# Summing the experts' rows into x by small products on chip, in a one-core decoder layer with 32 experts

## The chip, the core and the metric

The kernel runs on one core of a Trainium2 chip, as one program. The metric is the device time of one execution in microseconds (us); the number that counts is the median of several runs. The profile is of one further execution.

## What is computed

One inference step of a decoder layer for 264 tokens (256 of a prompt, 8 samples) with 1024 channels: a projection, an RWKV-7 branch and an attention branch, their merge into `x`, and then a layer of experts. Each token goes to 4 of 32 experts, and the 4 results, weighted, are added to `x`; a last norm gives `y`. The first part is not touched by the change. The second, cut to what matters, with all numbers in float32:

```python
def clamped_swiglu(u):
    glu = jnp.minimum(u[..., :D_FF], SWIGLU_LIMIT)
    lin = jnp.clip(u[..., D_FF:], -SWIGLU_LIMIT, SWIGLU_LIMIT)
    return glu * jax.nn.sigmoid(SWIGLU_ALPHA * glu) * (lin + 1.0)
...
    logits = (x @ w_router).astype(jnp.float32) + b_router.astype(jnp.float32)
    top_val, top_e = lax.top_k(logits, TOP_K)
    top_w = jax.nn.softmax(top_val, axis=-1).astype(h.dtype)
...
    def expert_chunk(args):
        xc, e = args
        return clamped_swiglu(xc @ w_up[e] + b_up[e]) @ w_down[e] + b_down[e]
    ys = lax.map(expert_chunk, (xs, chunk_e)).reshape(slots, D_MODEL)
    out = jax.ops.segment_sum(ys * slot_w[:, None], slot_tok, num_segments=n + 1)[:n]
...
    return x + moe_ffn(rms_norm(x, norm_ffn), w_router, b_router, w_up, b_up, w_down, b_down)
...
    y_prompt = rms_norm(xp, norm_final)
    y_sample = rms_norm(xs, norm_final)
```

Each expert has an upper weight of 1024x2048 (8 MB) and a lower one of 1024x1024 (4 MB).

## The kernel before

The engines run programs of their own and meet at semaphores. The layer of experts has four blocks of code, one behind the other, with all engines meeting between them.

`route` norms `x`, finds the 4 experts of each token, and gives each (token, choice) a slot: 64 slots to an expert (`SLOTS`), and further tiles of 64 for experts with more tokens, up to 16. A product with one-hot matrices (`hit`, `cell`) turns this into a table of slots by tiles; `src_row` has the row of the normed `h` (in memory) that a slot reads, `dst_row` the row of `scratch["choice"]` (also in memory, 4 rows to a token) that it writes. A row is handled as two halves of 512 elements, so a tile of 64 slots by 1024 channels is 128 partitions by 512. `route` also loads the biases, the first upper weight and the first two lower ones.

`first_tiles` goes through the 32 experts. SyncE streams the weights into `ring`: 8 slots of 1 MB for the upper weight, which are refilled as soon as TensorE has used them (`up_used`), and 2 x 4 slots for the lower ones (`down_used`). GpSimd gathers the rows of the next expert by an indirect transfer (`gather`), and writes the result of the last one by another (`scatter`). TensorE's order is written out by hand:

```python
with pe.Fori(1, NEXP // 2) as pair:
    up(2 * pair, True)
    turn_x(2 * pair + 1)
    down(2 * pair - 1, pair - 1, 1, True)
    up(2 * pair + 1, True)
    turn_x(2 * pair + 2)
    down(2 * pair, pair, 0, True)
```

`up(e)` multiplies the 64 rows by the 8 chunks of the upper weight (`L2039`), each into both column halves of the array, with `turn_h(e - 1)` (`L2026`) ahead of chunk 4, and adds the bias by a product of a one-hot `pick_up` with the bias table (`L2045`). `turn_x` (`L2020`) transposes the gathered rows. `down` multiplies by the lower weight (`L2057`) and adds its bias (`L2062`). VectorE's `tile(e)` clamps the two halves of the upper result (`L1996`, `L1997`), and makes `h`. ScalarE copies the transposed rows and the sigmoid, and `rows(e)` (`L1971`) copies the lower result from bank 4 to `y`, which the scatter (`L1941`) reads.

`further_tiles` loads a count `overflow` on every engine (`L2093`); where it is 0, as in this input, a branch jumps over the code. `finish` then loads the rows of `choice` back, adds them to `x` with their weights `top_w` on VectorE (`L2233`, 12 steps), takes the sums of squares on ScalarE (`L2221`), the roots, and writes `x` times the gain out (`L2244`).

## Time and profile before

| | us |
|---|---|
| median of 3 runs | 1611.16 (1606.93 to 1612.17) |
| the profiled execution | 1601.41 |
| its span, first to last instruction | 1599.6 |
| TensorE products busy | 1341.8 (84%) |
| VectorE busy | 365.2 (23%) |
| ScalarE busy | 201.3 (13%) |
| GpSimd busy | 140.0 (9%) |
| bytes moved by the DMA engines | 488.81 MB, mean 306 GB/s |

Busy times are sums over all stages, and the stages differ: the front part (to about 533 us) computes with little traffic, then comes `route`, and from about 571 us on the experts. A float32 product shows as two records of TensorE (PE) and two weight loads (PEld). In rows of time the first number is the start, the second the duration, both in us; square brackets hold the idle time of that engine ahead of the row, and what ended it. POOL is GpSimd, DVE is VectorE, ACT is ScalarE, SP is SyncE; a q behind an engine's name means its sequencer.

### The profile page before, as it was taken

The page shows a single profiled execution, that of the slowest core. Times are in us where ns is not written, and L with a number is a line of the kernel's source. Part 1 is how long each engine was busy: PE and PEld are TensorE (multiplying, and loading weights), DVE is VectorE, ACT ScalarE, POOL GpSimd, SP SyncE. Part 2 cuts the span into 40 slices and gives each one's busy share as a digit, 9 for nine tenths or more (in the row PEclk, how much of TensorE's full clock was granted, in tenths as well). Part 3 has the DMA queues.
Part 4 walks back from the last instruction along what each step waited for, and adds up shares of the span by engine and source line. Part 5 has one row for each costly group of instructions (what it writes and reads, how often), then busy time and mean ns, then how long its engine had stood idle before and what let it go on. Part 6 is the DMA issues. An engine that isn't in the chain of part 4 may idle for free. (4 is left out here: it accounts for less than half of the span.)

```text
span 1599.6 us, 21367 instructions
## 1 busy us (share of the span) xinstructions
PE 1341.8 (84%) x8262; PEld 665.5 (42%) x8263; DVE 365.2 (23%) x766; ACT 201.3 (13%) x432; POOL 140.0 (9%) x213
## 2 busy tenths in 40 slices
PE   6998889998889669988888888888888888888870
PEld 5887867786778523322222222222222222222220
DVE  2456473432341521101000100100010010001004
ACT  2221122122210201100000000000000000000001
POOL 1002040320000000000000000000000000000000
PEclk9999999899799669999999999999999999999995
DMA  5425083363272699999999999999999999999934
GB/s 168 129 84 136 4 242 124 108 234 149 106 197 66 240 366 417 417 416 415 418 418 415 418 418 416 416 418 417 415 418 418 415 416 418 416 415 417 418 135 150
DMA packets 142768, 488.81 MB, mean 306 GB/s; under 512 B 18926, under 2 KB 67296, under 8 KB 109328
## 3 DMA queue, kind: packets, MB, share of 16 engines
q1 hardware_dynamic: 131992, 457.55, 73.1%
q0 software_dynamic: 10320, 29.91, 5.2%
q8 instruction: 42, 0.69, 0.2%
q10 hardware_dynamic: 400, 0.55, 0.1%
q14 instruction: 14, 0.11, 0.0%
HBM read 483.57 MB, written 16.95 MB: 313 GB/s over the span
## 5 line engine op out<-in xcount | busy, mean ns | idle before, releaser
L2039 PE MATMUL bank<-ex_ring,ex_work 128*64 128x512 f32 x2048 | 492.2, 606 | 125.9 <-DMA ex_ring<-in_w_up 124.4
L2039 PEld LDWEIGHTS bank<-ex_ring,ex_work 128*64 128x64 f32 x2048 | 128.9, 137 | 466.0 <-DMA ex_ring<-in_w_up 280.0
L2057 PE MATMUL bank<-ex_ring,ex_work 128*64 128x512 f32 x1024 | 226.8, 595 | 0.7 <-ACT ex_work L1961 0.7
L1996 DVE TENSOR_SCALAR ex_work<-bank 128x512 f32<-128x512 f32 x32 | 22.1, 691 | 690.3 <-PE bank L2045 690.3
L2057 PEld LDWEIGHTS bank<-ex_ring,ex_work 128*64 128x64 f32 x1024 | 70.7, 137 | 134.0 <-issue 133.1
L498 PE MATMUL bank<-hT,w_group 128*128 128x264 f32 (+1 forms) x400 | 92.7, 394 | 0.7 <-DVE hT L398 0.7
L1941 POOL DMA_INDIRECT scratch_choice<-ex_work,ex_di x32 | 33.4, 1043 | 666.3 <-ACT ex_work L1971 666.3
L498 PEld LDWEIGHTS bank<-hT,w_group 128*128 128x128 f32 (+1 forms) x400 | 76.1, 191 | 16.6 <-DVE hT L398 1.1
L1293 PE MATMUL bank<-hT,w_cmp 128*128 128x264 f32 x256 | 68.2, 417 | 5.4 <-DMA w_cmp<-in_w_in 5.4
L1957 ACT ACTIVATE ex_work<-bank 128x512 f32<-128x512 f32 x33 | 19.7, 597 | 399.2 <-PE bank L2020 399.2
L2045 PE MATMUL bank<-ex_bias,ex_pick_up 32*64 32x512 f32 x256 | 61.8, 600 | 0.0
L1961 ACT ACTIVATE ex_work<-bank 128x512 f32<-128x512 f32 x32 | 19.1, 597 | 301.7 <-PE bank L2026 301.7
L1293 PEld LDWEIGHTS bank<-hT,w_cmp 128*128 128x128 f32 x256 | 50.5, 206 | 14.0 <-DMA w_cmp<-in_w_in 5.5
L1971 ACT ACTIVATE ex_work<-bank 128x512 f32<-128x512 f32 x32 | 19.1, 597 | 225.1 <-PE bank L2062 225.1
L2007 DVE COPY ex_pick_down<-ex_pick 32x64 f32 x31 | 5.7, 183 | 182.9 <-PE bank L2062 182.9
L1933 POOL DMA_INDIRECT ex_work<-scratch_h,ex_si x33 | 34.5, 1046 | 42.0 <-POOL ex_si L1928 24.3
L2062 PE MATMUL bank<-ex_bias,ex_pick_down 32*64 32x512 f32 x128 | 34.4, 613 | 0.0
L2045 PEld LDWEIGHTS bank<-ex_bias,ex_pick_up 32*64 32x64 f32 x256 | 15.0, 131 | 44.6 <-issue 44.6
L2020 PE MATMUL bank<-masks,ex_work 128*128 128x128 f32 x132 | 22.1, 291 | 9.6 <-DMA ex_work<-scratch_h,ex_si 9.5
L1670 PE MATMUL bank<-mixed,sel_rows 128*128 128x264 f32 x128 | 28.7, 387 | 1.5 <-DVE mixed L1644 1.5
L2020 PEld LDWEIGHTS bank<-masks,ex_work 128*128 128x128 f32 x132 | 14.1, 143 | 35.9 <-issue 24.3
L1670 PEld LDWEIGHTS bank<-mixed,sel_rows 128*128 128x128 f32 x128 | 24.2, 190 | 6.0 <-DVE mixed L1644 1.9
(464 smaller groups left out, 1229.4 us busy)
## 6 DMA issues: line engine op xcount, KB each, us to landing
ex_ring<-in_w_up SPq DMA_DIRECT2D x256, 1024.0 KB, 21.3
ex_ring<-in_w_down SPq DMA_DIRECT2D x256, 512.0 KB, 20.0
w_group<-in_w_in SPq DMA_DIRECT2D x12, 1024.0 KB, 5.4
w_cmp<-in_w_in SPq DMA_DIRECT2D x8, 1024.0 KB, 7.6
sel_rows<-in_w_out SPq DMA_DIRECT2D x8, 512.0 KB, 7.2
choice_rows<-scratch_choice SPq DMA_DIRECT2D x2, 2048.0 KB, 7.4
out_win_s<-in_state_win_kv POOLq DMA_DIRECT2D x1, 4088.0 KB, 24.9
x<-in_x_prompt SPq DMA_DIRECT2D x4, 512.0 KB
```

The costliest lines, as they stand in the source:

```text
L498: mm = mmul(banks[2 + i % 4][0:n, 0:T], w[:, g % 3, kc, c:c + n], hT[:, kc, :], start=(kc == 0), stop=(kc == KD - 1))
L1293: mm = mmul(gate_bank(t)[:, 0:T], w[:, t // 2 % 2, kc, P * (t % 2):P * (t % 2) + P], C["hT"][:, kc, :], start=(kc == 0), stop=(kc == KD - 1))
L1670: mm = mmul(banks[m % 2][:, 0:T], sel[:, c, m // 4, m % 4, P:256], mix[:, c, :], start=(c == 0), stop=(c == KD - 1))
L1933: pool.indirect_dma_start(B["xg"][:], None, halves(scratch["h"]), bass.IndirectOffsetOnAxis(ap=B["si"][:, 0:1], axis=0), bounds_check=last ...
L1941: pool.indirect_dma_start(halves(scratch["choice"]), bass.IndirectOffsetOnAxis(ap=B["di"][:, 0:1], axis=0), B["y"][:], None, bounds_check= ...
L1957: nc.scalar.activation(B["xT"][:].rearrange("p a b -> p (a b)"), banks[6][:], ACT.Copy).then_inc(S["xT_ready"], 1)
L1996: nc.vector.tensor_scalar(g[:], banks[0][:], 7.0, None, ALU.min).then_inc(S["g_ready"], 1)
L2020: mm = nc.tensor.transpose(banks[6][:, P * k:P * k + P], B["xg"][:, P * k:P * k + P], ident)
L2039: mm = mmul(banks[n // 2][lo:lo + SLOTS, :], B["xT"][:, k % 4, SLOTS * (k // 4):SLOTS * (k // 4) + SLOTS], B["ring"][:, k, 512 * n:512 * n ...
L2045: mm = mmul(banks[n // 2][lo:lo + SLOTS, :], B["pick_up"][:], B["bias"][:, 512 * n:512 * n + 512], start=False, stop=True)
L2057: mm = mmul(banks[4][SLOTS * n:SLOTS * n + SLOTS, :], B["hT"][:, k % 4, SLOTS * (k // 4):SLOTS * (k // 4) + SLOTS], B["ring"][:, 8 + 4 * h ...
L2062: mm = mmul(banks[4][SLOTS * n:SLOTS * n + SLOTS, :], B["pick_down"][:], B["bias"][:, 2 * FF + 512 * n:2 * FF + 512 * n + 512], start=Fals ...
```

## The change

The rows of an expert are no longer written to memory and read back. The table of `route` now gives each slot its token and its weight (`slot_tw`, from `dest` and `top_w`), for which the weights are normed earlier in `route`. In `first_tiles` VectorE makes for each expert a matrix `back` of slots by tokens, 128 x 384, that holds the slot's weight where slot and token meet (`back(e)`: `iota` compared with the slot's token, times its weight). TensorE multiplies `y` by it (`comb`): for each of three tiles of tokens two products of 64 rows, one for each half of the channels, into two banks; VectorE adds the six results to `x` (`adds`). `comb(e - 2)` stands ahead of chunk 2 of `up(e)`, and `turn_h` and `turn_x` wait for sums whose banks (7, 6) they write. The last two experts use other banks. `scatter`, `choice`, `dst_row` and `finish` are gone; the last norm stands behind the branch in the block of `further_tiles`, and the gain is loaded at the start of `first_tiles`. The tables of biases and picks are loaded twice, into partitions 0 to 31 and 32 to 63, and the four bias products of `up` take their rows from both and go in the order 0, 2, 1, 3.

```diff
                 def _(sp):
-                    sp.dma_start(B["bias"][:, 0:2 * FF], a["b_up"][0]).then_inc(b_in, 16)
-                    sp.dma_start(B["bias"][:, 2 * FF:3 * FF], a["b_down"][0]).then_inc(b_in, 16)
-                    sp.dma_start(B["pick"][:], a["c_pick"]).then_inc(b_in, 16)
+                    for i in range(2):
+                        es = slice(NEXP * i, NEXP * i + NEXP)
+                        sp.dma_start(B["bias"][es, 0:2 * FF], a["b_up"][0]).then_inc(b_in, 16)
+                        sp.dma_start(B["bias"][es, 2 * FF:3 * FF], a["b_down"][0]).then_inc(b_in, 16)
+                        sp.dma_start(B["pick"][es, :], a["c_pick"]).then_inc(b_in, 16)
...
-                    for j in range(2):
-                        step(tt_(cell[:, :, :, j, 0:NEXP], oh[:], dest[:, :, :, j].unsqueeze(3).to_broadcast([P, 3, TOPK, NEXP]), ALU.mult))
+                    step(tt_(cell[:, :, :, 0, 0:NEXP], oh[:], dest[:, :, :, 0].unsqueeze(3).to_broadcast([P, 3, TOPK, NEXP]), ALU.mult))
+                    dve.wait_ge(ex, 3)
+                    for t, (_, n) in enumerate(TILES):
+                        step(nc.vector.reciprocal(tsum[0:n, t:t + 1], tsum[0:n, t:t + 1]))
+                        step(ts_(top_w[0:n, t, :], top_w[0:n, t, :], tsum[0:n, t:t + 1], None, ALU.mult))
+                    step(tt_(cell[:, :, :, 1, 0:NEXP], oh[:], top_w[:].unsqueeze(3).to_broadcast([P, 3, TOPK, NEXP]), ALU.mult))
                     dve.wait_ge(rkd, 1)
...
-                    dve.wait_ge(ex, 3)
-                    for t, (_, n) in enumerate(TILES):
-                        step(nc.vector.reciprocal(tsum[0:n, t:t + 1], tsum[0:n, t:t + 1]))
-                        step(ts_(top_w[0:n, t, :], top_w[0:n, t, :], tsum[0:n, t:t + 1], None, ALU.mult))
+                    for t in range(3):
+                        step(ts_(B["iota"][:, P * t:P * t + P], num[:, 0:P], 2.0, float(2 * P * t + 1), ALU.mult, ALU.add))
...
-                    step(ts_(empty[:], b7, 0.0, 1e6, ALU.is_equal, ALU.mult))
-                    step(stt(rows_f[:], b7, num[:, 2 * P:2 * P + 1], empty[:], ALU.add, ALU.add))
-                    step(nc.vector.tensor_copy(src_row[:], rows_f[:, 0, :]))
-                    step(nc.vector.tensor_copy(dst_row[:], rows_f[:, 1, :]))
+                    step(ts_(empty[:], b7[:, 0, :], 0.0, 1e6, ALU.is_equal, ALU.mult))
+                    step(stt(rows_f[:], b7[:, 0, :], num[:, 2 * P:2 * P + 1], empty[:], ALU.add, ALU.add))
+                    step(nc.vector.tensor_copy(src_row[:], rows_f[:]))
+                    step(nc.vector.tensor_copy(slot_tw[:].rearrange("p c j -> p j c"), b7))
...
+                    sp.dma_start(gain[:], bass.AP(a["norm_final"].tensor, 0, [[0, P], [1, D]])).then_inc(g_in, 16)
...
-                    def scatter(e, n):
-                        nc.gpsimd.tensor_copy(B["di"][:], dst_row[:, bass.ds(e, 1)]).then_inc(S["idx"], 1)
-                        pool.wait_ge(S["idx"], n)
-                        pool.wait_ge(S["y_ready"], e + 1)
-                        pool.nop(nofuse=True)
-                        pool.indirect_dma_start(halves(scratch["choice"]), bass.IndirectOffsetOnAxis(ap=B["di"][:, 0:1], axis=0), B["y"][:], None,
-                                                bounds_check=last_choice, oob_is_err=False).then_inc(S["y_out"], 16)
-                        pool.wait_ge(S["y_out"], 16 * (e + 1))
-
                     step(nc.gpsimd.memset(B["xg"][:], 0.0))
                     gather(0, 1, False)
                     gather(1, 2, True)
                     with pool.Fori(1, NEXP) as e:
-                        gather(e + 1, 2 * e + 1, True)
-                        scatter(e - 1, 2 * e + 2)
-                    scatter(NEXP - 1, 2 * NEXP + 1)
+                        gather(e + 1, e + 2, True)
...
                     def rows(e, wait):
                         act.wait_ge(S["down_done"], e + 1)
                         if wait:
-                            act.wait_ge(S["y_out"], 16 * e)
+                            act.wait_ge(S["comb"], 3 * e)
                         nc.scalar.activation(B["y"][:], banks[4][:], ACT.Copy).then_inc(S["y_ready"], 1)
...
+                    def back(e):
+                        nc.vector.tensor_copy(B["tw"][:], slot_tw[:, bass.ds(e, 1), :].rearrange("p c j -> p (c j)")).then_inc(S["tw_read"], 1)
+                        dve.wait_ge(S["tw_read"], e + 1)
+                        nc.vector.tensor_scalar(B["back"][:], B["iota"][:], B["tw"][:, 0:1], B["tw"][:, 1:2], ALU.is_equal, ALU.mult).then_inc(S["back_ready"], 1)
+
+                    def adds(e, wait, last):
+                        if wait:
+                            dve.wait_ge(S["added"], 6 * e)
+                        for i, (t, bank) in enumerate(last_banks if last else sum_banks):
+                            n = TILES[t][1]
+                            dve.wait_ge(S["comb"], 3 * e + i // 2 + 1)
+                            dst = x[0:n, t, 512 * (i % 2):512 * (i % 2) + 512]
+                            nc.vector.tensor_tensor(dst, banks[bank][0:n, :], dst, ALU.add).then_inc(S["added"], 1)
...
+                    back(0)
                     tile(0, False)
-                    with dve.Fori(1, NEXP) as e:
+                    tile(1, True)
+                    adds(0, False, False)
+                    back(1)
+                    tile(2, True)
+                    with dve.Fori(3, NEXP) as e:
+                        adds(e - 2, True, False)
+                        back(e - 1)
                         tile(e, True)
+                    adds(NEXP - 2, True, True)
+                    back(NEXP - 1)
+                    adds(NEXP - 1, True, True)
+                    dve.wait_ge(S["added"], 6 * NEXP)
 
                 @block.tensor
...
+                    def comb(e, wait, last):
+                        pe.wait_ge(S["y_ready"], e + 1)
+                        pe.wait_ge(S["back_ready"], e + 1)
+                        if wait:
+                            pe.wait_ge(S["added"], 6 * e)
+                        for i, (t, bank) in enumerate(last_banks if last else sum_banks):
+                            hs = slice(SLOTS * (i % 2), SLOTS * (i % 2) + SLOTS)
+                            mm = mmul(banks[bank], B["back"][hs, P * t:P * t + P], B["y"][hs, :], start=True, stop=True)
+                            if i % 2:
+                                mm.then_inc(S["comb"], 1)
+
+                    def up(e, wait, back):
                         pe.wait_ge(S["xT_ready"], e + 1)
                         if wait:
                             pe.wait_ge(S["u_read"], e)
                         for k in range(KD):
+                            if back and k == 2:
+                                comb(e - 2, back > 1, False)
+                            if back and k == 4:
+                                pe.wait_ge(S["added"], 6 * (e - 2) + 1)
                             if wait and k == 4:
                                 turn_h(e - 1)
                             pe.wait_ge(ring_in[k], 16 * (e + 1))
...
-                        for n in range(4):
-                            lo = SLOTS * (n % 2)
-                            mm = mmul(banks[n // 2][lo:lo + SLOTS, :], B["pick_up"][:], B["bias"][:, 512 * n:512 * n + 512], start=False, stop=True)
+                        for n in (0, 2, 1, 3):
+                            lo, es = SLOTS * (n % 2), slice(NEXP * (n // 2), NEXP * (n // 2) + NEXP)
+                            mm = mmul(banks[n // 2][lo:lo + SLOTS, :], B["pick_up"][es, :], B["bias"][es, 512 * n:512 * n + 512], start=False, stop=True)
                         mm.then_inc(S["up_done"], 1)
...
                     turn_h(NEXP - 1)
+                    comb(NEXP - 2, True, True)
                     down(NEXP - 1, NEXP // 2 - 1, 1, True)
+                    comb(NEXP - 1, True, True)
...
+                    act.wait_ge(x_ok.sem, 1)
+                    for t, (_, n) in enumerate(TILES):
+                        if t:
+                            act.wait_ge(sq, t)
+                        nc.scalar.activation(sq_out[0:n, :], x[0:n, t, :], ACT.Square, accum_out=ss[0:n, t:t + 1]).then_inc(sq, 1)
+                    act.wait_ge(ms, 3)
+                    for t, (_, n) in enumerate(TILES):
+                        nc.scalar.activation(ss[0:n, t:t + 1], ss[0:n, t:t + 1], ACT.Sqrt).then_inc(root, 1)
 
...
+                    step = stepper(dve, dve_chain)
+                    step(nc.vector.memset(ss[:], 0.0), x_ok)
+                    for t, (_, n) in enumerate(TILES):
+                        dve.wait_ge(sq, t + 1)
+                        nc.vector.tensor_scalar(ss[0:n, t:t + 1], ss[0:n, t:t + 1], 1.0 / D, NORM_EPS, ALU.mult, ALU.add).then_inc(ms, 1)
+                    dve.wait_ge(root, 3)
+                    for t, (_, n) in enumerate(TILES):
+                        step(nc.vector.reciprocal(ss[0:n, t:t + 1], ss[0:n, t:t + 1]))
+                        nc.vector.scalar_tensor_tensor(x[0:n, t, :], x[0:n, t, :], ss[0:n, t:t + 1], gain[0:n, :], ALU.mult, ALU.mult).then_inc(y_ok, 1)
...
-                    for t, (t0, n) in enumerate(TILES):
-                        sp.dma_start(rows[0:n, t], scratch["choice"][TOPK * t0:TOPK * (t0 + n), :].rearrange("(t k) d -> t k d", k=TOPK)).then_inc(r_in[t], 16)
-                    sp.dma_start(gain[:], bass.AP(a["norm_final"].tensor, 0, [[0, P], [1, D]])).then_inc(g_in, 16)
...
-                    for t, (_, n) in enumerate(TILES):
-                        dve.wait_ge(r_in[t], 16)
-                        for k in range(TOPK):
-                            ins = stt(x[0:n, t, :], rows[0:n, t, k, :], top_w[0:n, t, k:k + 1], x[0:n, t, :], ALU.mult, ALU.add)
-                            if k < TOPK - 1:
-                                step(ins)
-                        ins.then_inc(x_ok, 1)
...
         experts()
-        finish()
         with nc.Block() as block:
```

TensorE's rows for one expert of the loop, before (`ex_ring` is the weights, `ex_work` the turned rows and all other work tiles):

```order
L2039 MATMUL bank<-ex_ring,ex_work 64x512 x16
L2026 MATMUL bank<-masks,ex_work 128x128 x4
L2039 MATMUL bank<-ex_ring,ex_work 64x512 x16
L2045 MATMUL bank<-ex_bias,ex_pick_up 64x512 x4
L2018 ISA
L2020 MATMUL bank<-masks,ex_work 128x128 x4
L2051 REGISTER_ALU
L2053 REGISTER_ALU
L2057 MATMUL bank<-ex_ring,ex_work 64x512 x16
L2062 MATMUL bank<-ex_bias,ex_pick_down 64x512 x2
```

The same place in the changed kernel, up to the bias of the upper half:

```order
L2079 MATMUL bank<-ex_ring,ex_work 64x512 x8
L2055 REGISTER_ALU
L2058 ISA
L2061 MATMUL bank<-ex_work,ex_back 128x512 x6
L2079 MATMUL bank<-ex_ring,ex_work 64x512 x8
L2073 REGISTER_ALU
L2051 MATMUL bank<-masks,ex_work 128x128 x4
L2079 MATMUL bank<-ex_ring,ex_work 64x512 x16
L2085 MATMUL bank<-ex_bias,ex_pick_up 64x512 x4
```

The six products of `comb` now split the first half of `up`; what follows is as before. TensorE's last rows of the block, before:

```order
L2026 MATMUL bank<-masks,ex_work 128x128 x4
L2057 MATMUL bank<-ex_ring,ex_work 64x512 x16
L2062 MATMUL bank<-ex_bias,ex_pick_down 64x512 x2
L1892 UNCONDITIONAL_BRANCH
```

And of the changed kernel:

```order
L2051 MATMUL bank<-masks,ex_work 128x128 x4
L2061 MATMUL bank<-ex_work,ex_back 128x512 x6
L2097 MATMUL bank<-ex_ring,ex_work 64x512 x16
L2102 MATMUL bank<-ex_bias,ex_pick_down 64x512 x2
L2061 MATMUL bank<-ex_work,ex_back 128x512 x6
L1899 UNCONDITIONAL_BRANCH
```

One `comb` stands ahead of the last lower product and one behind it. On VectorE the end of the block, which had no row behind the loop, is now:

```order
L2004 TENSOR_TENSOR x<-bank,x 8x512 x2
L2004 TENSOR_TENSOR x<-bank,x 128x512 x4
L1993 COPY ex_tw<-slot_tokens 128x2
L1995 TENSOR_SCALAR ex_back<-ex_iota,ex_tw 128x384
L2004 TENSOR_TENSOR x<-bank,x 8x512 x2
L2004 TENSOR_TENSOR x<-bank,x 128x512 x4
L1899 UNCONDITIONAL_BRANCH
```

Two sets of six adds to `x` were appended, with the matrix of the last expert between them.

## Rows read from the trace of the kernel before

**Rows 1.** The page: the span, and the DMA engines' share in 40 slices.
```profile
span 1599.6 us, 21367 instructions
...
DMA  5425083363272699999999999999999999999934
```

**Rows 2.** Windows: the loop's start, and the loop.
```profile
core 0: us, PE busy (x) PEld busy (x) DVE busy (x) ACT busy (x) POOL busy (x), PEclk, DMA share, GB/s
...
580.00:600.00 20.00, 19.07 (x77) 5.97 (x76) 0.78 (x2) 0.80 (x2) 1.22 (x2) 0.85 0.83 322
...
661.50:1530.00 868.50, 743.97 (x3266) 215.07 (x3264) 82.46 (x168) 64.65 (x112) 70.22 (x114) 1.00 1.02 416
```

**Rows 3.** The software queue: packets, MB, share; 661.5 to 1530, then 1015.3 to 1022.4.
```profile
q0 software_dynamic: 4560, 7.73, 2.4%
...
q0 software_dynamic: 80, 0.11, 4.1%
```

**Rows 4.** DMA issues, 1005.3 to 1036.33: count, size, median us to landing.
```profile
ex_ring<-in_w_up SPq DMA_DIRECT2D x9, 1024.0 KB, 22.7
```

**Rows 5.** Timeline of VectorE: the clamp of two experts, 17 apart.
```profile
1005.30 0.69 DVE L1996 TENSOR_SCALAR ex_work<-bank 128x512 f32<-128x512 f32 x1 [21.93 <-PE bank L2045]
...
1532.79 0.69 DVE L1996 TENSOR_SCALAR ex_work<-bank 128x512 f32<-128x512 f32 x1 [21.64 <-PE bank L2045]
```

**Rows 6.** Timeline of TensorE for an expert whose weights have landed.
```profile
600.61 7.09 PE L2039 MATMUL bank<-ex_ring,ex_work 128*64 128x512 f32 x32 [0.85 <-ACT ex_work L1957]
...
615.23 1.93 PE L2045 MATMUL bank<-ex_bias,ex_pick_up 32*64 32x512 f32 x8
...
617.09 0.66 PE L2020 MATMUL bank<-masks,ex_work 128*128 128x128 f32 x4
...
624.70 1.07 PE L2062 MATMUL bank<-ex_bias,ex_pick_down 32*64 32x512 f32 x4
...
625.70 7.09 PE L2039 MATMUL bank<-ex_ring,ex_work 128*64 128x512 f32 x32
```

**Rows 7.** Timeline of TensorE in the front part: whole products, and products of 64 rows.
```profile
499.81 27.09 PE L1670 MATMUL bank<-mixed,sel_rows 128*128 128x264 f32 x121
...
229.38 2.06 PE L1068 MATMUL bank<-sel_rows,w_cmp 64*128 64x265 f32 x16
231.37 2.05 PE L1108 MATMUL bank<-masks,sel_rows 128*128 128x128 f32 x16
```

**Rows 8.** Groups by form: busy us, mean ns; an add from a bank to x.
```profile
L1651 DVE TENSOR_TENSOR x<-x,bank 128x512 f32<-128x512 f32 x4 | 2.6, 683 | 30.2 <-PE bank L1678 30.2
```

**Rows 9.** Timeline of the last experts, all engines.
```profile
1541.28 0.66 PE L2026 MATMUL bank<-masks,ex_work 128*128 128x128 f32 x4
...
1542.62 7.09 PE L2057 MATMUL bank<-ex_ring,ex_work 128*64 128x512 f32 x32 [0.69 <-ACT ex_work L1961]
...
1550.76 0.60 ACT L1971 ACTIVATE ex_work<-bank 128x512 f32<-128x512 f32 x1 [8.19 <-PE bank L2062]
1552.13 0.99 POOL L1941 DMA_INDIRECT scratch_choice<-ex_work,ex_di x1 [5.43 <-ACT ex_work L1971]
```

**Rows 10.** Lines L1892 and L2093: duration ns min/median/max, start of first and last.
```profile
L1892 POOLq DRAIN  x1: 5370/5370/5370, 1554.9 to 1554.9; - x1
...
L2093 PEldq COMPARE_BRANCH  x1: 3952/3952/3952, 1562.2 to 1562.2; - x1
L2093 DVEq COMPARE_BRANCH  x1: 67/67/67, 1562.2 to 1562.2; - x1
```

**Rows 11.** Timeline of the last norm: the squares of the first and last tile.
```profile
1579.21 1.06 ACT L2221 ACTIVATE final_sq<-x 128x1024 f32<-128x1024 f32 x1 [27.86 <-DVE x L2233]
...
1590.15 1.05 ACT L2221 ACTIVATE final_sq<-x 8x1024 f32<-8x1024 f32 x1 [3.96 <-DVE x L2233]
```

**Rows 12.** Timeline of VectorE in route.
```profile
553.88 0.22 DVE L1791 COPY rank<-bank 128x64 f32<-128x64 f32 x1 [2.66 <-PE bank L1864]
...
565.00 0.23 DVE L1828 TENSOR_SCALAR top_w<-top_w,top_sum 128x4 f32<-128x4 f32 x1
```

151 lines of the change are left out of this document (74 added, 77 removed).

## The prediction

> **What bounds the kernel now.** I read the page first: of the 1599.6 us, the last 60% of the slices show the DMA engines at 9 tenths and more [rows 1]. So I split the span into stages. Over 868.5 us of the experts' loop the DMA share is 1.02 at 416 GB/s, the granted clock is 1.00 (the 2.4 GHz level), and TensorE is busy for 744 us [rows 2]: the loop goes at the pace of the weight stream. The period says the same. Expert e's clamp `L1996` at 1005.30 and that of expert 31 at 1532.79 lie 17 experts apart, so one takes 31.03 us [rows 5]; the same sequence on TensorE where everything it needs has landed (from the upper product at 600.61 over both halves, bias, turn, lower product and its bias to the next at 625.70) takes 25.09 us [rows 6]. TensorE has 5.9 us to spare per expert. A 1 MB weight load lands 22.7 us after its issue [rows 4], which at 416 GB/s is some 9 MB in flight: a slot of the ring that is freed a few microseconds later does not empty the stream. After the stream comes a tail in which one engine waits for the other, and it is all on the path: the last `y` is ready at 1550.76 + 0.60 = 1551.36 [rows 9], and the span ends at 1599.6, 48.2 us later.
>
> **Part 1, the scatters leave the stream.** Each of 32 experts wrote its rows to memory with one indirect transfer, on the same 16 engines as the weights. In the 7.1 us that hold one such transfer its queue took 4.1% [rows 3]: 0.29 us of all engines. Over the loop the software queue took 2.4% of 868.5 us for 4560 packets; at 80 packets for a transfer (the count in the short stretch) that is 57 gathers and scatters of 0.37 us, and by bytes 7.73 MB / 57 at 416 GB/s gives 0.33 us [rows 2, 3]. I take 0.31 us, between the shares, since the windows' total share of 1.02 says that packets' times overlap a little. 30 of the 32 scatters lie in the full stream (the last two start at 1542 and later, when the weights have landed): **-9.3 us**, ends -8.7 and -11.0. The gathers stay. Gathers no longer queue behind scatters on GpSimd, which brings nothing, since no stretch of the loop waits for them.
>
> **Part 2, what TensorE gets more.** Six products of 64 rows by 128 columns, 512 elements each, in three pairs that stand on different halves of the rows and write different banks. No row of before has this size. The nearest has the same tile shape: 16 records (8 products) of 64x265 from 229.38 to 231.37, 0.249 us each, where whole 128x128 products of 264 take 27.09/121 x 2 = 0.448 us [rows 7]. So two halves run side by side at 0.497 us a pair; scaled from 265 to 512 elements that is 0.96 us, 2.9 us for three pairs, switching included. If they ran one after the other, 6 x 0.448 x 512/264 = 5.2 us. I take 2.9. The Trainium skill (TensorEngine Tiling (Array Packing), Tiling Modes) says that tiles run in parallel but that a change of the tiling mode drains the engine; that speaks against putting 64x128 products into the middle of 128x64 ones. The trace has that switch on both sides of its own 64-row products at no more than the 0.05 us a pair by which 0.497 us stands above 265/264 of 0.448 us, so by the row the drain is already in the sum, and by the rule nothing larger follows.
>
> The four bias products of the upper half go from two pairs (615.23 to 617.09, 1.86 us) to four tiles of 32 rows; if all four run together they take what the lower half's one pair takes, 1.00 us (624.70 to 625.70) [rows 6]: -0.86 us, at worst 0. So an expert costs TensorE 25.09 + 2.9 - 0.86 = 27.1 us, at worst 25.09 + 5.2 = 30.3, under the new period of about 30.7. Inside one `up` it fits too: a chunk of 1.05 MB arrives every 2.52 us and takes TensorE 13.96/8 = 1.75 us (600.61 to 615.23 less a turn of 0.66), so the five chunks from the fourth on win back 3.9 us, against 2.9 for `comb` and 0.7 for the turn. In the loop this part costs 0, hidden by the waits for weights; without that cover it would cost 2.0 us an expert.
>
> What is queued behind the new waits: `comb(e-2)` stands before chunk 2 of `up(e)`, and six chunks, the turn and the ring slots wait behind it. It needs `y` of e-2, which ScalarE copies in 0.6 us once the lower product is done [rows 9], while chunks 0 and 1 take at least 3.5 us; and the matrix `back`, which VectorE made a period earlier. The wait for the first sum at chunk 4 is behind 3.5 us of products, where the add takes 0.7 us [rows 8]. VectorE gets per expert six adds of 0.68 us and a comparison of 128x384 (at most 0.69 us, a 128x512 row's price), 4.9 us with the small copy. They stand in front of the clamps, but VectorE idles 21.9 us there [rows 5].
>
> **Part 3, the front.** `route` now loads the bias tables twice (0.4 MB) and `first_tiles` loads the gain (0.5 MB) ahead of the second expert: 2.2 us of stream in all, but between 580 and 600 us the DMA share is 0.83 [rows 2], 3.4 us of idleness before the loop's loads begin. Cost 0; 2.2 us if that cover were gone. On VectorE six steps of at most 0.23 us with their gaps (1.4 us) come before the wait for the ranks, where it idles 2.66 us [rows 12]; three small comparisons take their old place behind the table's products' start. Cost 0, at worst 1.
>
> **Part 4, the tail.** Before the last lower product TensorE now does `comb(30)`. Today the turn is at 1541.28 and the product begins at 1542.62; `comb` can begin when `y` is copied, about 1542.1, and ends 2.9 us later, so 2.4 us later than now; the bias gives 0.86 back: **+1.5 us**. Counting on from the old time of `y`, 1551.36: first pair 1.1 us, then six adds of 0.68 us, x complete at 1556.6. The scatter of 1552.13, GpSimd's drain of 5.37 us behind it, all of `choice_rows` and twelve VectorE steps are gone; GpSimd's last transfer is now a gather an expert earlier. From the end of that drain (1554.9 + 5.37 = 1560.3) through the clearing of semaphores and the test on `overflow` to VectorE's branch it is 2.0 us (1562.2 + 0.07) [rows 10]; with the small memset 2.3 us. I use that: the square of the first tile at 1558.9. From there the old chain with its three squares close together: two squares more at 1.25 us with their reads, then the 9.45 us from 1590.15 to the end [rows 11], 11.95 us: 1570.9 in place of 1599.6, **-28.7 us**.
>
> **Sum.** -9.3 + 1.5 - 28.7 = -36.5 us: span 1563.1. This execution had 1601.41 us, 1.8 around its span, and 9.75 less than the median of the runs, 1611.16 (it is below their lowest, 1606.93). I carry the difference over to the median: 1611.16 - 36.5 = 1574.7, rounded 1575.
>
> **The rivals.**
> - *A jump that waits for its instructions.* VectorE's branch over the further tiles took 0.07 us, TensorE's 3.95 us on the same line [rows 10]. ScalarE and VectorE make the same jump, VectorE's body gets longer, and what follows is now the norm, on the path. If one of the two pays 3.95 us: 1579. The Trainium skill (Runtime: NRT & Kernel Launch, Instruction fetch mechanics) says that a taken branch whose target is outside the two pages at hand waits for a fetch; the 3.95 us agree with it, and whether the target falls outside can't be read from the trace. Chance 0.13.
> - *The pairs run one after the other.* For it: no row of 512 elements. Against it: rows 7. The loop still hides 5.2 us, the tail pays 2 x 2.3 us: 1579. Chance 0.05.
> - *The stream gives nothing back.* If the scatters' writes went beside the reads for nothing, only the tail counts: 1611.16 + 1.5 - 28.7 = 1584. For it: shares above 1 say that packets' times are not exclusive. Against it: there is no idle time for them to hide in. Chance 0.10.
> - *The other side: `comb`'s wait holds TensorE.* If `y` or the sums came late in the middle of `up`, chunks 2 to 7 and their slots would wait each time, and TensorE would set the period. The tail's 27.2 us are used up when each of 31 experts loses 0.9 us against now, at a period of 31.9, so when `comb` waits for 4.8 us or more beyond its work. Then 1611 and above; at 6 us of waiting the period is 33.1 and the time 1611 - 27.2 + 31 x 2.1, some 1649. Against it: `y` has 2.8 us in hand. Chance 0.04.
>
> **How the numbers follow.** The forecast has 0.62, a loss of part of the tail to something not priced that ends within 0.3% of before 0.03, and a larger gain (a stream share of 0.37 us and less waiting) 0.03. 0.3% (4.8 us) is about what a measurement of this kernel can tell from no change. The range goes from 1563 (the low end of the stream price, and the profiled execution's offset not carried over in full) to 1589 (stream rival plus the serial pairs); it leaves out about 1 in 10. Faster: 0.62 + 0.13 + 0.05 + 0.10 + 0.03 = 0.93; same 0.03; slower 0.04.
>
> **What would show it.** Right: the clamps of two experts 30.7 us apart, DMA share still 1.02 at 416 GB/s, a wait of TensorE for `ex_ring` before chunk 7 of each `up`; the six products in about 2.9 us; x complete some 5 us after the last `y`, the first square 2.3 us later, 12 us from it to the end. Wrong: a TensorE wait for `ex_work` or for VectorE inside `up`; a period of 31.0 with less traffic; products of 0.87 us one after the other; a branch of 4 us on ScalarE or VectorE; a late first chunk after `route`.

## The result and the profile after

The changed kernel takes 1549.54 us (median of 4, 1547.12 to 1553.82) against 1609.41 us (1606.93 to 1612.17, 4 runs) for the kernel before: ratio 0.9645, 95% interval 0.9623 to 0.9667. That is 25 us below the 1575 forecast and outside its range. The profiled execution took 1549.87 us, its span 1548.1.

The page after, in the parts that answer to [rows 1]; the q lines are the DMA queues over the whole span:
```profile
span 1548.1 us, 22460 instructions
...
DMA  5424257075165099999999999999999999999991
...
q1 hardware_dynamic: 131832, 453.62, 73.6%
q0 software_dynamic: 7760, 25.58, 4.6%
```
The full slices look the same and are fewer. The windows of after that answer to [rows 2] (the loop is cut at 1490, since it ends earlier):
```profile
580.00:600.00 20.00, 14.93 (x56) 5.10 (x58) 0.00 (x0) 0.60 (x1) 1.41 (x3) 0.71 0.92 360
661.50:1490.00 828.50, 779.46 (x3574) 246.30 (x3572) 200.96 (x392) 64.66 (x112) 33.74 (x55) 0.99 1.02 425
```
The loop's stream, at the same full share, moves 425 GB/s, where it moved 416. No term of the prediction has such a change in it. The DMA view of the same window, 661.5 to 1490, of the kernel before (packets, MB, share of 16 engines):
```profile
q1 hardware_dynamic: 61798, 337.82, 99.4%
q0 software_dynamic: 4320, 7.47, 2.4%
```
and of the changed kernel:
```profile
q1 hardware_dynamic: 63914, 347.98, 100.5%
q0 software_dynamic: 2240, 3.76, 1.2%
```
The gathers and scatters halved, as forecast. But a weight byte got cheaper too: 0.994 x 828.5 / 337.82 = 2.438 us of all engines per MB before, 1.005 x 828.5 / 347.98 = 2.393 after. Below, this number is called the price of the stream. Weights fill the queue, so 1.9% off their price should be nearly 1.9% off the loop, an estimate of 17 us.

The first and the last clamp bound the loop in every run; the view of the second clamp's line says where it stands in the kernel before and in the changed one (32 of them, first and last start):
```profile
L1997 DVE TENSOR_SCALAR ex_work<-bank x32: 678/680/681, 599.8 to 1533.4; 128x512 f32<-128x512 f32 x32
```
```profile
L2009 DVE TENSOR_SCALAR ex_work<-bank x32: 680/681/682, 604.5 to 1508.2; 128x512 f32<-128x512 f32 x32
```
So the 51.5 us between the two spans are three parts: **front** 599.8 to 604.5, +4.7; **loop** 933.6 to 903.7, -29.9; **tail** 66.2 to 39.9, -26.3. The tables below use these parts.

An expert on TensorE in the changed kernel's timeline, which answers to [rows 6]:
```profile
1006.57 1.94 PE L2079 MATMUL bank<-ex_ring,ex_work 128*64 128x512 f32 x8 [1.08 <-DMA ex_ring<-in_w_up]
1008.98 1.94 PE L2079 MATMUL bank<-ex_ring,ex_work 128*64 128x512 f32 x8 [0.47 <-DMA ex_ring<-in_w_up]
1010.84 2.85 PE L2061 MATMUL bank<-ex_work,ex_back 64*128 64x512 f32 x12
1013.62 3.65 PE L2079 MATMUL bank<-ex_ring,ex_work 128*64 128x512 f32 x16
1017.20 0.66 PE L2051 MATMUL bank<-masks,ex_work 128*128 128x128 f32 x4
1017.79 5.37 PE L2079 MATMUL bank<-ex_ring,ex_work 128*64 128x512 f32 x24
1023.66 1.94 PE L2079 MATMUL bank<-ex_ring,ex_work 128*64 128x512 f32 x8 [0.50 <-DMA ex_ring<-in_w_up]
1025.53 1.09 PE L2085 MATMUL bank<-ex_bias,ex_pick_up 32*64 32x512 f32 x8
```
`comb` takes 2.85 us and waits for nobody, the four bias products take 1.09, and the only waits are for weights.

What an expert costs TensorE can be read where its weights lie ready, in the first experts of the loop. VectorE's clamps there:
```profile
648.25 0.69 DVE L2008 TENSOR_SCALAR ex_work<-bank 128x512 f32<-128x512 f32 x1 [9.68 <-PE bank L2085]
...
675.43 0.69 DVE L2008 TENSOR_SCALAR ex_work<-bank 128x512 f32<-128x512 f32 x1 [9.69 <-PE bank L2085]
```
The period is 27.18 us here, 27.1 in the forecast, against about 30.0 later, where the stream sets it: TensorE has some 2.8 us to spare for an expert.

The tail of the changed kernel, all engines, answers to [rows 9, 11]:
```profile
1527.85 0.60 ACT L1969 ACTIVATE ex_work<-bank 128x512 f32<-128x512 f32 x1 [10.47 <-PE bank L2102]
...
1528.50 2.85 PE L2061 MATMUL bank<-ex_work,ex_back 64*128 64x512 f32 x12 [0.70 <-ACT ex_work L1969]
...
1529.75 3.67 DVE L2004 TENSOR_TENSOR x<-bank,x 8x512 f32<-8x512 f32 x6 [7.30 <-PE bank L2061]
...
1536.37 1.06 ACT L2201 ACTIVATE ex_ring<-x 128x1024 f32<-128x1024 f32 x1 [7.92 <-DVE final_ss L2232]
...
1538.73 1.06 ACT L2201 ACTIVATE ex_ring<-x 8x1024 f32<-8x1024 f32 x1
```
and what stands between x complete (1533.42) and the first square, in the views of lines L1899 and L2146, answers to [rows 10]:
```profile
L1899 POOLq DRAIN  x1: 7608/7608/7608, 1479.4 to 1479.4; - x1
...
L1899 DVEq DRAIN  x1: 10/10/10, 1533.7 to 1533.7; - x1
...
L2146 PEldq COMPARE_BRANCH  x1: 3888/3888/3888, 1535.6 to 1535.6; - x1
L2146 DVEq COMPARE_BRANCH  x1: 67/67/67, 1535.7 to 1535.7; - x1
```
GpSimd drains 7.6 us, but from 1479.4, and is done 41 us before the last `y`. TensorE pays its 3.9 us at the branch and nobody waits for it. From the last `y` (1528.45) to the end it is 19.65 us, against 48.24.

### The profile page after: what moved, and what is told of

Its sections match the earlier page's. It is cut to its first block and busy times, and to the rows that moved or that the text cites. A ratio compares the mean times of both kernels' runs of the same rounds, so it can differ in the third digit from the quotient of the medians.

```text
span 1548.1 us, 22460 instructions
## 1 busy us (share of the span) xinstructions
PE 1392.6 (90%) x8646; PEld 701.9 (45%) x8647; DVE 485.4 (31%) x1015; ACT 201.6 (13%) x432; POOL 98.9 (6%) x149
## 5 line engine op out<-in xcount | busy, mean ns | idle before, releaser
L2079 PE MATMUL bank<-ex_ring,ex_work 128*64 128x512 f32 x2048 | 482.6, 614 | 51.1 <-DMA ex_ring<-in_w_up 49.5
L2079 PEld LDWEIGHTS bank<-ex_ring,ex_work 128*64 128x64 f32 x2048 | 139.1, 139 | 367.4 <-issue 267.7
L2097 PE MATMUL bank<-ex_ring,ex_work 128*64 128x512 f32 x1024 | 226.8, 595 | 0.0
L2004 DVE TENSOR_TENSOR x<-bank,x 128x512 f32<-128x512 f32 (+1 forms) x192 | 117.4, 671 | 197.8 <-PE bank L2061 197.8
L2097 PEld LDWEIGHTS bank<-ex_ring,ex_work 128*64 128x64 f32 x1024 | 70.7, 137 | 133.9 <-issue 133.9
L2061 PE MATMUL bank<-ex_work,ex_back 64*128 64x512 f32 x384 | 91.1, 606 | 0.9 <-ACT ex_work L1969 0.9
L2019 DVE COPY ex_pick_down<-ex_pick 64x64 f32 (+1 forms) x31 | 5.8, 187 | 181.8 <-PE bank L2102 181.8
L2061 PEld LDWEIGHTS bank<-ex_work,ex_back 64*128 64x128 f32 x384 | 34.4, 186 | 56.5 <-issue 54.5
L2085 PE MATMUL bank<-ex_bias,ex_pick_up 32*64 32x512 f32 x256 | 34.8, 613 | 0.0
L1670 PE MATMUL bank<-mixed,sel_rows 128*128 128x264 f32 x128 | 28.7, 387 | 1.5 <-DVE mixed L1644 1.5
```

The lines of the kernel that those rows point to most:

```text
L1670: mm = mmul(banks[m % 2][:, 0:T], sel[:, c, m // 4, m % 4, P:256], mix[:, c, :], start=(c == 0), stop=(c == KD - 1))
L2004: nc.vector.tensor_tensor(dst, banks[bank][0:n, :], dst, ALU.add).then_inc(S["added"], 1)
L2061: mm = mmul(banks[bank], B["back"][hs, P * t:P * t + P], B["y"][hs, :], start=True, stop=True)
L2079: mm = mmul(banks[n // 2][lo:lo + SLOTS, :], B["xT"][:, k % 4, SLOTS * (k // 4):SLOTS * (k // 4) + SLOTS], B["ring"][:, k, 512 * n:512 * n ...
L2085: mm = mmul(banks[n // 2][lo:lo + SLOTS, :], B["pick_up"][es, :], B["bias"][es, 512 * n:512 * n + 512], start=False, stop=True)
L2097: mm = mmul(banks[4][SLOTS * n:SLOTS * n + SLOTS, :], B["hT"][:, k % 4, SLOTS * (k // 4):SLOTS * (k // 4) + SLOTS], B["ring"][:, 8 + 4 * h ...
```

## The experiments

Two questions stood open. How much of the loop's 29.9 us belongs to the scatters? What made the weights cheaper? Theory A: the scatters' writes slow the reads around them, so the price falls with the scatters. Theory B: a scatter costs its own packets only, and the price fell for another reason.

**The scatters, three edits and a control.** `b0_same` is the kernel before, unchanged:

> The kernel before, unchanged, with a profile of its own. All theories: ratio 1.000, and a period of 31.0 us between two experts' clamps. The question is the price of a weight packet in the full stream: the first profile had 99.3% of 868.5 us for 353.84 MB, 2.44 us per MB, the changed kernel's 100.5% of 828.5 us for 347.98 MB, 2.39 us per MB. If the higher price belongs to this kernel it is there again; if it belonged to that one execution, it is 2.39 here and the period is 30.5.

`e1_before_no_scatter` takes the scatters out of the kernel before; `finish` then reads rows of `w_down` in place of the choices, so the output lacks the experts' sums:
```diff
-   pool.indirect_dma_start(halves(scratch["choice"]), ..., B["y"][:], None, ...).then_inc(S["y_out"], 16)
-   pool.wait_ge(S["y_out"], 16 * (e + 1))
...
-   act.wait_ge(S["y_out"], 16 * e)
```

> The kernel before without the 32 scatters (the rows of choice that the end adds up are read from w_down, so y is not the reference's); everything else, the norm's block too, stays. Theory A, the scatters slow the whole stream, also outside the microseconds in which their own packets move: period 30.1 us, 2.39 us per MB, 30 us less than before (ratio 0.981). Theory B, a scatter costs only its own packets and the rest of the gain comes from where something lies in memory or on chip: period 30.7 us, 2.44 us per MB, 10 us less (0.994).

`e2_after_scatter` puts a scatter of `y` per expert back into the changed kernel, beside the sums (it takes its rows from `src_row`, so as many rows and bytes as before go to other places of the table; over the whole span the software queue moves 10320 packets and 29.91 MB in both); `e3_after_choice_kept` only declares the table in memory again and writes 8 rows to it at the end:
```diff
+   scatter(e - 1)             # e2: behind gather(e + 1), and ScalarE's rows() waits for y_out again
...
+   sp.dma_start(scratch["choice"][0:TS, :], x[0:TS, 2, :])     # e3
```

> The changed kernel with a scatter of y per expert put back (same rows, same volume, into a table that nobody reads), sums on chip as before. Theory A: period 31.0 us, 2.44 us per MB, 30 us over the changed kernel (ratio to before 0.981). Theory B: period 30.4 us at 2.39 us per MB, 10 us over the changed kernel (0.969).

> The changed kernel with the table choice still declared in memory and 8 rows of it written once at the very end, so that tensors lie in memory as before. Theory A: as the changed kernel, 1550 us (ratio 0.963), 2.39 us per MB. Theory B in its form that the place of the tensors in memory does it: 2.44 us per MB, a period of 30.6 us, 1568 us (0.974).

Measured (medians in us; price in us/MB, from the queue's line as above; parts in us from the profiled execution):
```
                       median   ratio [95%]               price  front  loop   tail
b0_same                1606.72  0.9992 [0.9978, 1.0006]   2.438  604.2  933.6  68.1
e1_before_no_scatter   1589.41  0.9897 [0.9875, 0.9919]   2.440  602.3  920.8  61.0
e2_after_scatter       1569.68  0.9771 [0.9750, 0.9792]   2.395  603.7  917.4  43.7
e3_after_choice_kept   1553.17  0.9669 [0.9649, 0.9690]   2.393  607.0  903.5  40.6
```
The q lines of `e1_before_no_scatter`, 661.5 to 1490, behind that price:
```profile
q1 hardware_dynamic: 62718, 341.63, 100.6%
q0 software_dynamic: 2164, 3.76, 1.2%
```
Without scatters the old price stays, 2.440; with them put back the new price stays, 2.395. Theory A falls. What the scatters cost is what they add to the loop: 12.8 us taken out of the kernel before, 13.7 put into the changed one. (The tail of `e1_before_no_scatter` is 5.2 us shorter as well: its GpSimd drains 2.76 us from 1541.4, where it was 5.37 us from 1554.9, [rows 10].) The other half of the loop's gain, some 16 to 17 us, is there with scatters and without, and the table in memory has nothing to do with it.

**The place of the ring.** The control has the old price again, so the price belongs to the program and not to one execution. What else differs for the weights? The diff makes `dst_row` (one word for each of 48 chunks) into `slot_tokens` (two words). The tiles lie one behind the other in a partition, so all that come later move by 192 bytes: `ex_ring` from byte 54592, which is 64 past a multiple of 256, to 54784, a multiple of 512. (These bytes are the tiles' sizes added up, with the allocation's rounding; no trace shows them. The shifts of 192, 128 and 256 bytes are in the edits themselves.) Theory P: the place makes the packets quicker. Theory Q: it is what the engines do meanwhile. `f1_before_all_moved` only widens `dst_row`; `f2_before_ring_moved` only puts 192 unused bytes ahead of the ring:
```diff
-        dst_row = sb(ctx, "dst_row", [P, NCHUNK], U32)
+        dst_row = sb(ctx, "dst_row", [P, 2 * NCHUNK], U32)      # f1
...
             work = sb(moe, "ex_work", [P, 8, 512])
+            sb(moe, "ex_pad", [P, 48])                          # f2
```

> The kernel before with dst_row made twice as wide (only its first half is used), so that every on-chip tile behind it, ex_ring too, lies 192 bytes further on each partition, where the changed kernel has it; no instruction changes. Theory P (place): the weight packets are quicker where ex_ring begins at byte 54784 of a partition (a multiple of 512) than at 54592 (64 past a multiple of 128). It expects the changed kernel's price of the stream, 2.39 us/MB in place of 2.44 in the window of the loop, a period of 30.4 us in place of 31.0, and about 18 us off the whole: about 1589. Theory Q (the stream's price hangs on what the engines do meanwhile: the order on TensorE, the idle GpSimd queue) expects no change: 1607, 2.44 us/MB.

> The kernel before with an unused tile of 192 bytes between ex_work and ex_ring: only ex_ring and the small tiles behind it move, to the changed kernel's place. Theory P expects the same as from moving everything, about 1589 and 2.39 us/MB, since it lays the price at the ring's own place. If moving everything is worth something and this is not, it is another tile's place (ex_work, x, the front's tiles). Theory Q expects 1607.

`f3_after_ring_back` gives the ring its old place in the changed kernel, `f4_after_ring_plus_128` and `g1_after_ring_plus_256` move it on:
```diff
-        slot_tw = sb(ctx, "slot_tokens", [P, NCHUNK, 2])
+        sb(ctx, "slot_pad", [P, NCHUNK])              # f3; slot_tokens is laid behind the ring
...
+            sb(moe, "ex_pad", [P, 32])                # f4; [P, 64] in g1
```

> The changed kernel with slot_tokens laid behind the ring, and an unused tile of 192 bytes where dst_row was, so that ex_work and ex_ring lie as in the kernel before; no instruction changes. Theory P expects 2.44 us/MB, a period of about 30.6, and about 17 us more than the changed kernel: 1567. Theory Q expects no change: 1550, 2.39 us/MB.

> The changed kernel with an unused tile of 128 bytes ahead of ex_ring, which then begins at byte 54912: a multiple of 128, not of 256. Theory P in the form that any place that is a multiple of 128 is quick expects 1550 and 2.39 us/MB; in the form that 256 or 512 is wanted, about 1567 and 2.44 us/MB. Theory Q expects 1550.

> The changed kernel with an unused tile of 256 bytes ahead of ex_ring, which then begins at byte 55040 of a partition: a multiple of 256, not of 512. If 256 is what the weight packets want, 1550 and 2.39 us/MB, as the changed kernel; if 512, 1567 and 2.44 us/MB, as with 128 bytes more. No theory of mine tells these two apart beforehand.

```
                         ring at (mod 256)   median   ratio [95%]               price  front  loop   tail
f1_before_all_moved      54784 (0)           1591.26  0.9918 [0.9893, 0.9943]   2.393  597.6  917.5  66.3
f2_before_ring_moved     54784 (0)           1591.99  0.9909 [0.9887, 0.9931]   2.394  607.0  917.6  66.5
f3_after_ring_back       54592 (64)          1565.98  0.9751 [0.9731, 0.9771]   2.438  604.9  920.3  40.0
f4_after_ring_plus_128   54912 (128)         1567.77  0.9756 [0.9732, 0.9779]   2.437  610.2  918.8  39.9
g1_after_ring_plus_256   55040 (0)           1548.71  0.9638 [0.9611, 0.9666]   2.393  603.6  903.9  39.9
```
Two of the q1 lines, 661.5 to 1490, of `f2_before_ring_moved` and then of `f3_after_ring_back`:
```profile
q1 hardware_dynamic: 63113, 343.65, 99.3%
```
```profile
q1 hardware_dynamic: 62590, 341.52, 100.5%
```
192 unused bytes take 14 us off the kernel before (16.0 off its loop); the old place adds 16 to the changed one. Theory P holds, for the ring and the small tables behind it (f2 does as much as f1, and only the ring receives weights), and the bound is 256 bytes: 64 and 128 past it are equally slow, 256 is as quick as 512. By the shifts alone, 192 and 448 bytes on are quick and 0 and 320 slow, which no shorter pattern than 256 fits; other places were not tried. The traces' records of single packets, 661.5 to 1490, show the same: in the changed kernel a packet of 8 KB takes 309.1 ns on average and one of 4 KB 159.0, nearly all of them the same; before it is 314.3 and 162.7, and in `f4_after_ring_plus_128` 313.9 and 162.9. A packet to the slow place costs 4 to 5 ns more, at either size and at 64 or 128 bytes past. The two causes add up: 933.6 less 16.1 for the place (f1) and 12.8 for the scatters (e1) is 904.7, and the changed loop takes 903.7. The Trainium skill (DMA: Bandwidth & Descriptors, How a descriptor splits into AXI transactions) says that a descriptor is split into pieces of 256 bytes which start at multiples of 256, so that one of 8 or 4 KB which starts elsewhere takes a piece more. The runs agree with the bound. They do not agree with a size taken from its account, an estimate: 33 and 17 pieces in place of 32 and 16 are 4% more over these bytes; counted in beats of 32 bytes it is 1% more at 64 past and 2% at 128. The measured 1.9% is the same at both places. So the place as the cause is shown, and how a packet loses its 4 to 5 ns is not.

**How much TensorE has to spare.** `g2_after_comb_serial` was to make `comb` longer by taking its products half by half (its other line, not shown, lets the last three products signal VectorE):
```diff
-   for i, (t, bank) in enumerate(last_banks if last else sum_banks):
+   for j, i in enumerate((0, 2, 4, 1, 3, 5)):
+       t, bank = (last_banks if last else sum_banks)[i]
```

> The changed kernel with comb's six products in the order 0, 2, 4, 1, 3, 5, so that all but one pair of neighbours use the same row half and don't run side by side: a comb of 5.2 us or a little less in place of 2.9. The prediction's account (TensorE needs 27.1 us an expert and waits for the ring for the rest) puts this at nothing in the loop, a period of 30.1 us, and at about 2.3 us for each of the two comb behind the last turn: 1554. The rival reads TensorE's own waits for the ring, 31.7 us in 16 experts counted at every chunk, as 2 us of slack an expert, of which the trace lacks a part: then 0.3 us or more an expert shows, 10 us or more in all: 1564 or later.

Measured 1555.28 us, ratio 0.9684 [0.9651, 0.9717]; loop 904.6, tail 42.6. One `comb` of it in the loop, TensorE:
```profile
1011.99 3.81 PE L2062 MATMUL bank<-ex_work,ex_back 64*128 64x512 f32 x12
1015.72 3.65 PE L2080 MATMUL bank<-ex_ring,ex_work 128*64 128x512 f32 x16
1019.31 0.66 PE L2051 MATMUL bank<-masks,ex_work 128*128 128x128 f32 x4
1019.89 7.09 PE L2080 MATMUL bank<-ex_ring,ex_work 128*64 128x512 f32 x32
```
The reordered `comb` is 0.96 us longer, not 2.3, because the order did not make it serial. The records of `comb` on TensorE that fall in each stretch, in windows with `--tile ex_back`; first four stretches of this run's `comb`:
```profile
1011.98:1012.50 0.52, 0.51 (x1) 0.29 (x2) 0.00 (x0) 1.00 0.97 410
1012.50:1012.94 0.44, 0.44 (x2) 0.19 (x1) 0.00 (x0) 1.00 1.10 465
1012.94:1013.37 0.43, 0.43 (x3) 0.30 (x3) 0.00 (x0) 1.00 0.94 400
1013.37:1013.80 0.43, 0.43 (x4) 0.30 (x2) 0.00 (x0) 1.00 1.08 457
```
and of the changed kernel's:
```profile
1010.83:1011.37 0.54, 0.53 (x2) 0.30 (x4) 0.00 (x0) 1.00 1.04 440
1011.37:1011.80 0.43, 0.43 (x4) 0.19 (x2) 0.00 (x0) 1.00 0.99 419
```
A record is 0.59 us long, and the next one on the same half starts 0.43 us after it, so one half at work shows as two records in a stretch and both halves as four. In the changed kernel both halves work from the start. Here the second half's first record, of product 1, starts 0.97 us after the first half's, beside product 2, although products 2 and 4 stand ahead of it in the program (by the start times of the trace's records); from there both halves work side by side again. Twelve records of 0.43 us one behind the other would be 5.15 us, an estimate that agrees with the 5.2 of the prediction; no run had such a `comb`.

The loop hides the 0.96 us (+0.9 us in all of it): its first experts, whose weights lie ready, now lie 28.14 us apart in place of 27.18, and the later ones 30.0 as before; the wait of 0.50 us before the last chunk is gone. The tail grows by 2.7. The `comb` ahead of the last lower product adds its 0.96 us, and behind the last one the first add comes later:
```profile
1530.86 3.81 PE L2062 MATMUL bank<-ex_work,ex_back 64*128 64x512 f32 x12 [0.70 <-ACT ex_work L1969]
...
1533.82 3.67 DVE L2004 TENSOR_TENSOR x<-bank,x 8x512 f32<-8x512 f32 x6 [8.26 <-PE bank L2062]
```
That is 2.96 us after `comb` starts, where it was 1.25, so 1.71 more: VectorE waits for product 1, and had its signal only when product 4, ahead of it in the program, was done as well (its second record starts at 1533.11 and takes 0.59). Of the 6.6 us between the medians of this run and `g1_after_ring_plus_256` these parts explain 3.6. The rival that more than 10 us would show falls for 1 us an expert; the 2.3 us that I meant to add would still fit into the 2.8 to spare, which was not tried.

**Longer packets.** With the price of a byte now the lever, `h1_down_8k` loads `w_down` in rows of 8 KB in place of 4, and `h2_both_paired` also `w_up` in rows of 16:
```diff
-   sp.dma_start(B["ring"][:, slot, D * c:D * c + D], a["w_down"][0][..., r0:r0 + P, :] ...)        # twice a slot
+   sp.dma_start(B["ring"][:, slot, :], a["w_down"][0][bass.ds(e, 1), 256 * j:256 * j + 256, :]
+                .rearrange("e (p c) n -> (e p) (c n)", c=2))
...
-   nc.tensor.transpose(banks[7][:, P * k:P * k + P], B["h"][:, P * k:P * k + P], ident)
+   nc.tensor.transpose(banks[7][:, P * k:P * k + P], B["h"][:, 256 * (k // 2) + k % 2:256 * (k // 2) + 256:2], ident)
```

> The changed kernel with w_down loaded in rows of 8 KB: each partition takes two neighbouring rows of w_down (rows 2p and 2p + 1 of a block of 256) as one piece, one transfer for a ring slot in place of two, and turn_h takes every second column of h, so that the products see the same rows. In the changed kernel a packet of 4 KB takes about half as long as one of 8 KB and 5 ns more (the 512 KB transfers are slower a byte than the 1 MB ones). If a fixed time per packet is what a small packet costs more, 512 packets of 8 KB an expert in place of 1024 of 4 KB save about 0.29 us an expert, 9 us in all: 1541. If the transposes of strided columns are slower, or a slot landing later holds TensorE up, less, or no gain: 1550 or later.

> As with w_down in rows of 8 KB, and w_up paired in the same way: four transfers of 2 MB with 16 KB a partition for an expert in place of eight of 1 MB, turn_x taking every second column of xg. If a packet can be 16 KB, another 0.29 us an expert is saved: 1532. If a packet is cut at some smaller size, the same time as with w_down alone. Against it: TensorE gets w_up in steps of 2 MB, up(e + 1) can only start when two slots are free, and the first product of an expert waits for twice the data, so that the stream's own start after a stall is later: 1545 or more.

```
                 median   ratio [95%]               price  front  loop   tail
h1_down_8k       1547.89  0.9631 [0.9605, 0.9656]   2.367  609.5  898.6  39.9
h2_both_paired   1547.11  0.9615 [0.9582, 0.9648]   2.346  607.8  898.7  40.0
```
The first line behind this table (h1, 661.5 to 1490), with a quarter of the packets gone:
```profile
q1 hardware_dynamic: 48074, 350.07, 100.0%
```
Packets of 8 KB for `w_down` take another 1.1% off the price and 5.1 us off the loop, where 9 were expected. Pairing `w_up` lowers the price again and the loop not at all. The clamps tell where the gain goes: against `h1_down_8k` the 23 periods from the eighth expert on are 3.8 us shorter together, but the seven before them are 2.9 longer and the last one is 1.1 longer (30.53 in place of 29.46). So the quicker stream does shorten the middle, and the two ends of the loop take it back; which wait lengthens them was not followed. Against `g1_after_ring_plus_256` on the same chip the medians fall by 0.8 and 1.6 us only. The profiled executions of both had fronts 5.9 and 4.2 us longer than that of `g1_after_ring_plus_256`, by chance or not; that the whole is faster is not shown.

## Why the prediction was wrong

**The step that failed** is the sentence of the first paragraph that the loop goes at 416 GB/s, used as a constant in Part 1. The direction, the tail and the hidden parts came out as argued; the price of a weight byte was taken to be a property of the chip, when it was one of this program's layout, and the change altered the layout. The diff showed it: one tile got 192 bytes longer. I priced what the edit does to instructions and not what it does to the addresses of the tiles behind it. With the ring at its old place the changed kernel takes 1565.98 us (f3), inside the range of 1563 to 1589: without the shift of the ring, the measured time would have lain within it, 9 us under the forecast.

- *Part 1, the scatters:* the mechanism was right, the term too small. Forecast -9.3 us (0.31 each), at most -11.0; measured -12.8 (e1) and 13.7 (e2), 0.43 to 0.46 for each of 30. The halves of the software queue's line give 0.012 x 828.5 / 28 = 0.36 us for one gather; the low end of my reading rested on a window of 7 us. The 0.07 to 0.1 us beyond a transfer's own packets were not explained.
- *The weights' price:* forecast unchanged, measured -16.1 us (f1), 16.6 back (f3). This is the term that was missing.
- *Part 2:* `comb` 2.85 us (forecast 2.9), bias 1.09 (1.00), hidden in the loop. TensorE's 27.1 us for an expert came out at 27.18. The forecast period of 30.7 was 30.06 (1026.68 to 1507.62, 16 experts), which the two points above account for. The bound for serial products, 5.2 us, was never reached in a run; twelve records at their measured 0.43 us say 5.15.
- *Part 3, the front:* the cost of 0 holds where the change is. `route` begins at 533.52 before and 538.83 after, in code that is the same in both, and from there to the first clamp it is 66.3 and 65.7 us. Over the 14 profiles that beginning lies anywhere from 531.24 to 544.22:
```profile
531.24 0.33 SPq L1733 DMA_DIRECT2D ex_bias<-in_b_up  x1
```
```profile
544.22 0.33 SPq L1736 DMA_DIRECT2D ex_bias<-in_b_up  x1
```
  (f1 and f4, SyncE). Part of it is TensorE's granted clock: before 520 us, f1 spends 51.2 us at the lower level and f4 64.9, which would be worth at most 6.9 of the 13.0 us. What else moves it, and what makes the clock fall, was not followed.
- *Part 4, the tail:* forecast +1.5 and -28.7 with 0.86 taken off at the bias, measured by its own points: last clamp to `y` 18.57 to 20.83, `y` to the end 48.24 to 19.65, so +2.3 and -28.6. First add 1.30 us after `y` (1.1), x complete 4.97 after it (5.2), first square 2.95 later (2.3), 11.7 from it to the end (11.95). This is the step to copy: the old tail read row by row, and each gap of the new one built from a row of the old.
- *The offset:* I carried over that the profiled execution lay 9.75 us under the median. It was chance, not a property of the kernel: that execution's front was 4 to 5 us shorter than usual, and the first median was high (later ones are 1606 to 1607). The changed kernel's profiled execution is 0.3 us above its median. So some 10 us of the miss are bad luck with this offset, and the +4.7 us of the front hid part of the rest. Of the 25 us between forecast and result, about 15 lie between the forecast span of 1563.1 and the measured 1548.1 (-16.1 place, -3.5 scatters, +4.7 front, +0.9 tail, -1.0 not assigned), and the other 10 are this.

Of the rivals, no jump stalled ScalarE (54 ns) or VectorE (67 ns), the pairs ran side by side, the stream gave back more than forecast and not nothing, and `comb` waited for `y` only in the tail: 0.19 us for the last expert but one, and 0.70 for the last, for which nothing else is left to do until its `y` is there. None of them, and neither end of the range, had a change of the stream's price in it: a bound taken from rows of before holds only what the change leaves alone.

## What to carry to other kernels

Where a stream of weights sets the pace, look up where its buffer begins in a partition, and keep that at a multiple of 256 bytes: 192 unused bytes were worth 14 us in 1606 here. When a change adds or widens any tile, work out which streams' buffers move, and price it before the rest; and when an edit gains more than its instructions can explain, pad the tile back before giving the credit to the edit. A stage that one engine's queue fills is best checked by its price for a byte, since that number stays the same in every kernel which leaves the stream alone, while the span varies with its front.

## What was not expected of the hardware

- The ring's place: 2.438 us/MB at 64 or 128 bytes past a multiple of 256, 2.393 at a multiple, from 661.5 to 1490 us, whatever ran beside it (twelve profiles, the two with longer packets left out).
- A scatter by a list of rows cost the full stream 0.43 to 0.46 us, 20 to 29% more than the queue's share says (0.36).
- Six products of 64 rows and 512 columns take 2.85 us in pairs on the two row halves. Written half by half they take 3.81 us and still run side by side for the most part: by the trace's start times a product on the free half began while two that stood ahead of it in the program were still to be done on the other, and its signal came only behind theirs.
- The front of the program, the same instructions each time (in some runs with the tiles 192 bytes further on), ended at points up to 13 us apart in 14 executions, while the loop's 933.6 us agreed to 0.1 us in two executions of the kernel before.
